# Moving the experts' tiles to other distances from the weights, modulo 256 bytes

## The chip, the cores and the metric

The kernel runs on one core of one Trainium2 chip. The metric is device time in microseconds (us) of one execution. Five units work side by side and meet only at semaphores: TensorE (PE; its weight load, LDWEIGHTS, is shown apart as PEld), VectorE (DVE), ScalarE (ACT), GpSimd (POOL) and SyncE (SP), which issues most of the DMA transfers. Tiles lie in the on-chip memory SBUF, 128 partitions wide; a tile's address is its byte offset inside a partition. Matmul results go to a second memory, `ps` in the code. In a matmul one operand, 128 by 128, is loaded first and stays (the stationary one); the other streams past it column by column (the moving one).

## The reference: what is computed

A decoder trunk of two layers is run for 256 prompt tokens and 32 sample tokens, 288 in all, of width 1024. Each layer mixes (gated DeltaNet heads beside a Conformer convolution) and then has a feed-forward part: layer 0 a dense SwiGLU of width 2816, layer 1 a choice of two among eight experts, each a SwiGLU of width 3584. The change touches only the experts:

```
def swiglu(x, wg, wu, wd):
    return (jax.nn.silu(x @ wg) * (x @ wu)) @ wd

# moe_swiglu(h, ...), cut
logits = h @ w_r + b_r;  probs = softmax(logits)
top_p, top_e = lax.top_k(probs, 2);  top_p = top_p / sum(top_p)
...                                   # assignments sorted by expert, blocks of 128 rows
yb = lax.map(expert_block, (xb, block_e))        # swiglu(xblk, wg[e], wu[e], wd[e])
contrib = yb[dest] * sp[:, None]
return segment_sum(contrib, stok, num_segments=n_tok)
```

All inputs are 32-bit floats.

## The kernel before, in words

**Weights.** All large weights come as units of 128 x 2048 floats (1 MB). SyncE loads them in a fixed order into six buffers `raw`. For most of them the product is taken in three parts, to keep 32-bit accuracy with the fast matmul type float32r: ScalarE rounds a unit into `whi` (L687), VectorE puts the remainder raw - whi into `wlo` (L1061), and TensorE adds up three products: high by high, high by low and low by high. `whi` and `wlo` have three buffers each.

**Before the experts.** In the input projection of layer 0's later units and of layer 1's, and in the dense feed-forward (L1702 to L1704), the weights are the stationary operand and the tokens' tiles `h_hi`, `h_lo`, `act_hi`, `act_lo` move, 288 columns at a time. Their 288-column slices start every 1152 bytes, so that they stand alternately at 0 and at 128 modulo 256. Other projections (L2048, L1885) and the sums of squares for the norms (L1747, stationary operand: the block of ones in `con`) use plain 32-bit matmuls of 288 columns.

**The experts.** Here the roles are turned round. For each expert, `gather` (L2173) fetches its rows: a 0/1 matrix `pe_sel` picks rows of `tok_hi` and `tok_lo` into `xe`, which is transposed and split into `ht_hi[q]` and `ht_lo[q]` (q changes with the expert). Then 42 units follow in the order g, g, u, u, d, d. In the loop of L2241 each unit gives four groups of three matmuls: the stationary operand is a 128 x 128 slice of the experts' rows, the moving one a slice of 512 columns of `whi` or `wlo`:

```
mm(ps[:, bank, :], a_hi[:, a], whi[u % NSPLIT][:, w], ...)    # L2244
mm(ps[:, bank, :], a_hi[:, a], wlo[u % NSPLIT][:, w], ...)    # L2245
mm(ps[:, bank, :], a_lo[:, a], whi[u % NSPLIT][:, w], ...)    # L2246
```

For g and u units `a_hi`, `a_lo` are `ht_hi[q]`, `ht_lo[q]`; for d units they are `at_hi[c % 2]`, `at_lo[c % 2]`, where c counts seven blocks of 512 hidden columns. Between them stand silu(g) (`sge`), the gated product (`ae`), its transposes (L2221) and its split into `at_hi` (ACT, L1031) and `at_lo` (DVE, L1632). The previous expert's result `ye_hi`, `ye_lo` is scattered back to the tokens through `pt_sel` (L2206, L2207) and added to `facc` (L1620). That is 8 experts of 42 units: 336 units and 4032 matmuls of 512 columns.

**What sets the order.** Every engine's program is written out by hand, with semaphores; there is no planner. TensorE needs a unit's `wlo` (semaphore `lo_split`), ScalarE a free `whi` (`unit_used`) and a landed `raw`.

**Addresses.** `at(name, offset, ...)` places a tile at a byte offset, `keep` packs tiles one behind the other. `raw`, `whi` and `wlo` are packed first, 8192 bytes each. `r0`, from which the experts' tiles are counted, lies 86272 bytes behind the first `whi`, and 86272 is 337 x 256. So an offset of `r0 + n` stands at n modulo 256 from the weights. All the experts' tiles have multiples of 256 there but `pos_e`, which stands at 128. `con`, which holds the constants, stands at 32. Slices taken from the tiles for a weight load are 512 bytes apart and those of the weights 2048 bytes, so they keep their tile's remainder.

Of the kernel before, what the change touches and what calls it, by code (L numbers as in the profile page):

```python
# [27 lines left out]
F32R = mybir.dt.float32r  # L28
# [6 lines left out]
P = 128  # L35
D = 1024
# [4 lines left out]
T = TP + TS  # L41
# [224 lines left out]
def program(nc, units, x_in, c_in, par_in, const_in, gdn_in, qst_in, cst_in,  # L266
            y_out, gdnp_out, gdns_out, qst_out, cst_out):
    ctx = ExitStack()
    with ctx:
# [5 lines left out]
        def at(name, offset, cols, dt=F32):  # L275
            return nc.alloc_sbuf_tensor_at(name, [P, cols], dt, offset=offset)
# [23 lines left out]
        r0 = cursor[0]  # L300
# [51 lines left out]
        act_hi = at("act_hi", r0 + 18432, FT * T, F32R)  # L352
        act_lo = at("act_lo", r0 + 43776, FT * T, F32R)

        tok_hi = at("tok_hi", r0 + 36864, 3 * D, F32R)
        tok_lo = at("tok_lo", r0 + 49152, 2 * D, F32R)
        facc = at("facc", r0 + 61440, KD * T)

        ht_hi = [at(f"ht_hi{i}", r0 + 70656 * i, D, F32R) for i in range(2)]
        ht_lo = [at(f"ht_lo{i}", r0 + 70656 * i + 4096, D, F32R) for i in range(2)]  # L360
        xe = at("xe", r0 + 78848, D)
        sge = [at(f"sge{i}", r0 + 8192 + 2048 * i, 512) for i in range(2)]
        ae = [at(f"ae{i}", r0 + 12288 + 2048 * i, 512) for i in range(2)]
        at_hi = [at(f"at_hi{i}", r0 + 16384 + 16128 * i, 512, F32R) for i in range(2)]
        at_lo = [at(f"at_lo{i}", r0 + 18432 + 16128 * i, 512, F32R) for i in range(2)]
        ye_hi = at("ye_hi", r0 + 20480, D, F32R)
        ye_lo = at("ye_lo", r0 + 24576, D, F32R)
        pe_sel = at("pe_sel", r0 + 28672, 3 * P, F32R)
        pt_sel = [at(f"pt_sel{i}", r0 + 30208 + i * 52736, T, F32R) for i in range(2)]
        pos_e = at("pos_e", r0 + 31360, T, F32R)  # L370
        ones_r = at("ones_r", r0 + 84480, P, F32R)
        wgt_parts = at("wgt_parts", r0 + 85248, 6 * NE, F32R)
        assert r0 + 89088 <= base + room, (base + room - r0)
# [2013 lines left out]
```

## Time and profile before

| | |
|---|---|
| time of the kernel, median of 3 runs | 1764.25 us (1761.23 to 1768.3) |
| the profiled execution | 1764.47 us |
| its span, first to last instruction | 1762.7 us |
| PE / PEld / DVE / ACT busy | 1719.2 / 1442.9 / 1370.3 / 1033.9 us |
| first and last of the experts' L2244 start at | 758.8 and 1744.4 us |
| granted TensorE clock, mean | 0.983 of 2.4 GHz |

The page shows one execution. Matmuls overlap in the pipeline and the end of each is modelled, so the time from one matmul's start to the next one's start says how fast TensorE goes; the duration printed for one does not. A PE that is "busy" throughout can still be slower than it might be.

### The profile page before, as it was taken

The numbers are of one execution on the slowest core, as the hardware profiler recorded it, in microseconds if no ns is written. First come the engines' busy times: TensorE is split into PE (matmuls) and PEld (weight loads), VectorE is DVE, ScalarE is ACT, GpSimd is POOL, SyncE is SP. The second block draws the span as 40 slices with busy tenths as digits, with TensorE's granted clock in tenths as the row PEclk, the third lists the DMA queues.
The fourth block names the chain that finished last, engine by engine and source line by source line (L and its number), as shares of the span: only waits on it lengthen the run. The fifth ranks groups of instructions, "written<-read, shape, count | busy, mean of one in ns | idle before, by whom it ended". The sixth has DMA issues, their size and how long they took to land.

```text
span 1762.7 us, 25478 instructions
## 1 busy us (share of the span) xinstructions
PE 1719.2 (98%) x9464; PEld 1442.9 (82%) x9464; DVE 1370.3 (78%) x1627; ACT 1033.9 (59%) x989; POOL 77.7 (4%) x97
## 2 busy tenths in 40 slices
PE   6999999999999999799999999999999999999997
PEld 3878978999978798578888888888888888888886
DVE  2698565554348975678898898998988988988998
ACT  3345424443333544167777777777777777777775
POOL 0122100000011130100000000000000000000000
PEclk9999999999999999899999999999999999999999
DMA  9776047444476510379999999999999999999997
GB/s 384 297 307 217 25 173 291 166 164 168 144 283 267 202 56 31 120 278 344 358 362 351 359 368 347 359 356 339 376 359 353 350 360 344 376 346 371 351 366 268
DMA packets 73386, 499.49 MB, mean 283 GB/s; under 512 B 8096, under 2 KB 8224, under 8 KB 15296
## 3 DMA queue, kind: packets, MB, share of 16 engines
q1 hardware_dynamic: 69728, 481.16, 72.3%
q0 software_dynamic: 3552, 16.87, 2.5%
q8 instruction: 72, 1.18, 0.3%
q14 instruction: 34, 0.28, 0.0%
HBM read 485.95 MB, written 12.05 MB: 283 GB/s over the span
## 4 chain that ended last, share of the span: by engine, by line
PE 91%; DVE 6%; DMA 2%; issue 1%; ACT 0%; SPq 0%; DVEq 0%
PE ps L2244 17%; PE ps L2246 17%; PE ps L2245 17%; PE ps L1702 5%; PE ps L1704 5%; PE ps L1703 5%; PE ps L1885 3%; PE ps L2048 3%; PE ps L1713 2%; DMA raw<-units 2%; DVE yc L1131 1%; PE ps L2221 1%; PE ps L2188 1%; PE ps L1723 1%; PE ps L1793 1%; PE ps L1808 1%
## 5 line engine op out<-in xcount | busy, mean ns | idle before, releaser
L1061 DVE TENSOR_TENSOR wlo<-raw,whi 128x2048 fp32r<-128x2048 f32 x384 | 876.6, 2291 | 184.6 <-ACT whi L687 184.5
L687 ACT ACTIVATE whi<-raw 128x2048 fp32r<-128x2048 f32 x384 | 735.6, 1918 | 256.4 <-PE ps L2246 203.3
L2244 PE MATMUL ps<-whi,ht_hi 128*128 128x512 f32 x896 | 355.5, 397 | 1.7 <-DVE ht_lo L1606 1.7
L2246 PE MATMUL ps<-whi,ht_lo 128*128 128x512 f32 x896 | 349.3, 390 | 0.0
L2245 PE MATMUL ps<-wlo,ht_hi 128*128 128x512 f32 x896 | 349.3, 390 | 0.0
L2246 PEld LDWEIGHTS ps<-whi,ht_lo 128*128 128x128 f32 x896 | 168.1, 188 | 35.8
L2244 PEld LDWEIGHTS ps<-whi,ht_hi 128*128 128x128 f32 x896 | 168.3, 188 | 34.9 <-issue 1.9
L2245 PEld LDWEIGHTS ps<-wlo,ht_hi 128*128 128x128 f32 x896 | 168.5, 188 | 31.5
L2244 PE MATMUL ps<-whi,at_hi 128*128 128x512 f32 x448 | 175.2, 391 | 0.0
L2246 PE MATMUL ps<-whi,at_lo 128*128 128x512 f32 x448 | 174.4, 389 | 0.0
L2245 PE MATMUL ps<-wlo,at_hi 128*128 128x512 f32 x448 | 174.4, 389 | 0.0
L1702 PE MATMUL ps<-h_hi,whi 128*128 128x288 f32 x560 | 167.2, 299 | 0.0
L1703 PE MATMUL ps<-h_lo,whi 128*128 128x288 f32 x560 | 165.2, 295 | 0.0
L1704 PE MATMUL ps<-h_hi,wlo 128*128 128x288 f32 x560 | 164.7, 294 | 0.0
L1702 PEld LDWEIGHTS ps<-h_hi,whi 128*128 128x128 f32 x560 | 104.9, 187 | 9.8 <-issue 9.7
L1704 PEld LDWEIGHTS ps<-h_hi,wlo 128*128 128x128 f32 x560 | 105.5, 188 | 0.0
L1703 PEld LDWEIGHTS ps<-h_lo,whi 128*128 128x128 f32 x560 | 105.1, 188 | 0.1
L1131 DVE SCALAR_TENSOR_TENSOR yc<-cpad,par,yc 128x256 f32<-128x256 f32 x240 | 103.9, 506 | 0.0
L2246 PEld LDWEIGHTS ps<-whi,at_lo 128*128 128x128 f32 x448 | 84.1, 188 | 17.8
L2244 PEld LDWEIGHTS ps<-whi,at_hi 128*128 128x128 f32 x448 | 84.1, 188 | 16.7
L2245 PEld LDWEIGHTS ps<-wlo,at_hi 128*128 128x128 f32 x448 | 84.1, 188 | 16.6
L2048 PE MATMUL ps<-hf,raw 128*128 128x288 f32 x352 | 91.6, 421 | 2.8 <-DVE hf L1111 2.8
(347 smaller groups left out, 2012.9 us busy)
## 6 DMA issues: line engine op xcount, KB each, us to landing
raw<-units SPq DMA_DIRECT2D x447, 1024.0 KB, 6.4
raw<-units SPq DMA_DIRECT2D x16, 512.0 KB, 5.9
sst<-gdn_in POOLq DMA_DIRECT2D x8, 512.0 KB, 6.2
gdns_out<-sst POOLq DMA_DIRECT2D x8, 512.0 KB, 4.3
qst_out<-qpad POOLq DMA_DIRECT2D x2, 1890.0 KB, 10.4
cst_out<-cpad POOLq DMA_DIRECT2D x2, 1116.0 KB, 13.1
x<-x_in SPq DMA_DIRECT2D x1, 1152.0 KB, 9.1
y_out<-hf SPq DMA_DIRECT2D x2, 576.0 KB, 2.9
```

What stands on the lines that cost most here:

```text
L687: act.activation(whi[s % NSPLIT][:, :], raw[u % NRAW][:, :], ACT.Copy).then_inc(hi_split, 1)
L1061: dve.tensor_tensor(wlo[s % NSPLIT][:, :], raw[unit_of(s) % NRAW][:, :], whi[s % NSPLIT][:, :].bitcast(F32), ALU.subtract).then_inc(lo_spl ...
L1131: dve.scalar_tensor_tensor(y, cp3[:, c, j:j + TP], w, y, ALU.mult, ALU.add).then_inc(tap_prompt, 1)
L1702: mm(out, w_hi, x_hi, start=start, stop=False)
L1703: mm(out, w_hi, x_lo, start=False, stop=False)
L1704: return mm(out, w_lo, x_hi, start=False, stop=stop)
L1713: last = mm(ps[32 * k:32 * k + 32, bank, :], cst3[:, 4 * half + k], raw[u % NRAW][:, k * 512:(k + 1) * 512], start=(half == 0), stop=(half ...
L1885: last = mm(ps[:, bank, 0:T], raw[u % NRAW][:, w], part, start=(k == 0), stop=(k == 3))
L2048: last = mm(ps[:, bank, 0:T], raw[u % NRAW][:, w], hf3[:, k], start=(k == 0), stop=(k == KD - 1))
L2244: mm(ps[:, bank, :], a_hi[:, a], whi[u % NSPLIT][:, w], start=(first and i == 0), stop=False)
L2245: mm(ps[:, bank, :], a_hi[:, a], wlo[u % NSPLIT][:, w], start=False, stop=False)
L2246: last = mm(ps[:, bank, :], a_lo[:, a], whi[u % NSPLIT][:, w], start=False, stop=(end and i == 3))
```

## The change

The offsets of the expert stage's tiles (14 names, some with two buffers) become others; nothing else is edited. The sizes stay, and so does the order of every engine's instructions: on PE, DVE, ACT, POOL and SP the two programs have the same instructions in the same order. Tiles that stay are `facc`, `ones_r`, `wgt_parts` and all tiles of the stages before the experts.

```
--- before.py
+++ after.py
@@ -352,22 +352,22 @@
         act_hi = at("act_hi", r0 + 18432, FT * T, F32R)
         act_lo = at("act_lo", r0 + 43776, FT * T, F32R)
 
-        tok_hi = at("tok_hi", r0 + 36864, 3 * D, F32R)
-        tok_lo = at("tok_lo", r0 + 49152, 2 * D, F32R)
+        tok_hi = at("tok_hi", r0 + 37888, 3 * D, F32R)
+        tok_lo = at("tok_lo", r0 + 50176, 2 * D, F32R)
         facc = at("facc", r0 + 61440, KD * T)
 
-        ht_hi = [at(f"ht_hi{i}", r0 + 70656 * i, D, F32R) for i in range(2)]
-        ht_lo = [at(f"ht_lo{i}", r0 + 70656 * i + 4096, D, F32R) for i in range(2)]
-        xe = at("xe", r0 + 78848, D)
-        sge = [at(f"sge{i}", r0 + 8192 + 2048 * i, 512) for i in range(2)]
-        ae = [at(f"ae{i}", r0 + 12288 + 2048 * i, 512) for i in range(2)]
-        at_hi = [at(f"at_hi{i}", r0 + 16384 + 16128 * i, 512, F32R) for i in range(2)]
-        at_lo = [at(f"at_lo{i}", r0 + 18432 + 16128 * i, 512, F32R) for i in range(2)]
-        ye_hi = at("ye_hi", r0 + 20480, D, F32R)
-        ye_lo = at("ye_lo", r0 + 24576, D, F32R)
-        pe_sel = at("pe_sel", r0 + 28672, 3 * P, F32R)
-        pt_sel = [at(f"pt_sel{i}", r0 + 30208 + i * 52736, T, F32R) for i in range(2)]
-        pos_e = at("pos_e", r0 + 31360, T, F32R)
+        ht_hi = [at(f"ht_hi{i}", r0 + (192, 70880)[i], D, F32R) for i in range(2)]
+        ht_lo = [at(f"ht_lo{i}", r0 + (4384, 75104)[i], D, F32R) for i in range(2)]
+        xe = at("xe", r0 + 79200, D)
+        sge = [at(f"sge{i}", r0 + 8512 + 2048 * i, 512) for i in range(2)]
+        ae = [at(f"ae{i}", r0 + 12608 + 2048 * i, 512) for i in range(2)]
+        at_hi = [at(f"at_hi{i}", r0 + (16800, 33280)[i], 512, F32R) for i in range(2)]
+        at_lo = [at(f"at_lo{i}", r0 + (19168, 35328)[i], 512, F32R) for i in range(2)]
+        ye_hi = at("ye_hi", r0 + 21216, D, F32R)
+        ye_lo = at("ye_lo", r0 + 25312, D, F32R)
+        pe_sel = at("pe_sel", r0 + 29408, 3 * P, F32R)
+        pt_sel = [at(f"pt_sel{i}", r0 + (30944, 83296)[i], T, F32R) for i in range(2)]
+        pos_e = at("pos_e", r0 + 32096, T, F32R)
         ones_r = at("ones_r", r0 + 84480, P, F32R)
         wgt_parts = at("wgt_parts", r0 + 85248, 6 * NE, F32R)
         assert r0 + 89088 <= base + room, (base + room - r0)
```

Distance from the weights, modulo 256 bytes:

| tile | before | after |
|---|---|---|
| ht_hi[0], ht_lo[0] | 0, 0 | 192, 32 |
| ht_hi[1], ht_lo[1] | 0, 0 | 224, 96 |
| at_hi[0], at_lo[0] | 0, 0 | 160, 224 |
| at_hi[1], at_lo[1] | 0, 0 | 0, 0 |
| ye_hi, ye_lo | 0, 0 | 224, 224 |
| pt_sel[0], pt_sel[1] | 0, 0 | 224, 96 |
| pe_sel, pos_e | 0, 128 | 224, 96 |
| xe, sge[0], sge[1], ae[0], ae[1] | 0 | 96, 64, 64, 64, 64 |
| tok_hi, tok_lo | 0, 0 | 0, 0 |

All the new offsets are multiples of 32.

## Rows read from the trace of the kernel before

**Rows 1.** The page, parts 1 and 2: busy time; clock, DMA and GB/s by slice

```profile
PE 1719.2 (98%) x9464; PEld 1442.9 (82%) x9464; DVE 1370.3 (78%) x1627; ACT 1033.9 (59%) x989; POOL 77.7 (4%) x97
...
PEclk9999999999999999899999999999999999999999
DMA  9776047444476510379999999999999999999997
GB/s 384 297 307 217 25 173 291 166 164 168 144 283 267 202 56 31 120 278 344 358 362 351 359 368 347 359 356 339 376 359 353 350 360 344 376 346 371 351 366 268
```

**Rows 2.** The page, part 4: the chain that ended last

```profile
PE 91%; DVE 6%; DMA 2%; issue 1%; ACT 0%; SPq 0%; DVEq 0%
PE ps L2244 17%; PE ps L2246 17%; PE ps L2245 17%; PE ps L1702 5%; PE ps L1704 5%; PE ps L1703 5%; PE ps L1885 3%; PE ps L2048 3%; PE ps L1713 2%; DMA raw<-units 2%; DVE yc L1131 1%; PE ps L2221 1%; PE ps L2188 1%; PE ps L1723 1%; PE ps L17
```

**Rows 3.** Stretches: busy us (x instructions) by engine, PE clock, DMA share, GB/s

```profile
core 0: us, PE busy (x) PEld busy (x) DVE busy (x) ACT busy (x) POOL busy (x), PEclk, DMA share, GB/s
300.00:400.00 100.00, 100.00 (x752) 100.00 (x752) 48.91 (x48) 47.53 (x51) 0.00 (x0) 1.00 0.47 168
575.00:596.00 21.00, 21.00 (x88) 16.43 (x88) 20.93 (x48) 8.55 (x27) 3.49 (x4) 1.00 0.34 112
1596.00:1607.00 11.00, 11.00 (x50) 9.13 (x49) 9.78 (x8) 7.68 (x4) 0.00 (x0) 1.00 0.93 357
...
757.00:1735.00 978.00, 976.35 (x4493) 808.22 (x4493) 872.99 (x604) 716.85 (x489) 0.00 (x0) 1.00 0.94 354
```

**Rows 4.** The page, part 5: busy us, mean ns of one, idle us before

```profile
L1061 DVE TENSOR_TENSOR wlo<-raw,whi 128x2048 fp32r<-128x2048 f32 x384 | 876.6, 2291 | 184.6 <-ACT whi L687 184.5
L687 ACT ACTIVATE whi<-raw 128x2048 fp32r<-128x2048 f32 x384 | 735.6, 1918 | 256.4 <-PE ps L2246 203.3
L2244 PE MATMUL ps<-whi,ht_hi 128*128 128x512 f32 x896 | 355.5, 397 | 1.7 <-DVE ht_lo L1606 1.7
...
L2244 PEld LDWEIGHTS ps<-whi,ht_hi 128*128 128x128 f32 x896 | 168.3, 188 | 34.9 <-issue 1.9
...
L2244 PE MATMUL ps<-whi,at_hi 128*128 128x512 f32 x448 | 175.2, 391 | 0.0
...
L2048 PE MATMUL ps<-hf,raw 128*128 128x288 f32 x352 | 91.6, 421 | 2.8 <-DVE hf L1111 2.8
```

**Rows 5.** Timeline, PE, an undisturbed stretch of the expert stage

```profile
start us, us, engine line op out<-in xcount [idle before <-releaser]
...
1596.44 0.39 PE L2246 MATMUL ps<-whi,ht_lo 128*128 128x512 f32 x1
1596.67 0.39 PE L2244 MATMUL ps<-whi,at_hi 128*128 128x512 f32 x1
1596.89 0.39 PE L2245 MATMUL ps<-wlo,at_hi 128*128 128x512 f32 x1
1597.12 0.39 PE L2246 MATMUL ps<-whi,at_lo 128*128 128x512 f32 x1
...
1598.71 0.39 PE L2244 MATMUL ps<-whi,at_hi 128*128 128x512 f32 x1
```

**Rows 6.** Timeline, PE, in the dense feed-forward part's stage

```profile
299.83 0.29 PE L1703 MATMUL ps<-h_lo,whi 128*128 128x288 f32 x1
299.97 0.29 PE L1704 MATMUL ps<-h_hi,wlo 128*128 128x288 f32 x1
...
301.04 0.29 PE L1703 MATMUL ps<-h_lo,whi 128*128 128x288 f32 x1
```

**Rows 7.** Timeline, PE, 32-bit matmuls: an input projection, and the sums of squares of a norm

```profile
574.10 23.20 PE L2048 MATMUL ps<-hf,raw 128*128 128x288 f32 x95
...
488.35 4.04 PE L1747 MATMUL ps<-sqx,con 128*128 128x288 f32 x16
```

**Rows 8.** Timeline, PE, the largest spacing that is common in the expert stage

```profile
783.16 0.40 PE L2244 MATMUL ps<-whi,at_hi 128*128 128x512 f32 x1
783.40 0.39 PE L2245 MATMUL ps<-wlo,at_hi 128*128 128x512 f32 x1
```

## The prediction

> **What bounds the kernel now.** Read the busy table and the slices first: PE is busy for 98% of the span, and the granted clock is at nine tenths or more in all slices but one [rows 1]. The chain of waits says the same with more weight: 91% of it is PE, and the three expert matmul lines L2244 to L2246 are 51% of the whole span [rows 2]. So the question is only how fast these matmuls follow each other. The groups by line show 0.0 to 1.7 us of idle time before them, while DVE (L1061) and ACT (L687) have 184.6 and 256.4 us of idle before their splits, most of it for each other or for PE [rows 4]. In the stretch of the experts, 978 us, PE is busy for 976.35, DVE for 873 (89%), and the DMA engines for 94% [rows 3]. PE binds; DMA and DVE are 6 and 11% behind it, which matters if PE gets faster.
>
> A busy PE may still be slowed by how it reads its operands, and this change can act only there. So take spacings, start to start, not the printed durations.
> - Experts, float32r, 512 columns: 1596.44 to 1598.71 us is ten spacings, 227 ns each [rows 5]; the 11 us stretch around it agrees, (11.00 + 0.39) / 50 = 228 [rows 3].
> - Token projections and the dense part, float32r, 288 columns: (100.00 + 0.29) / 752 = 133.4 ns [rows 3].
> - The two differ by 93.6 ns over 224 columns, 0.418 ns a column, which is 2.4 GHz at a granted clock of 1.00 [rows 3]. At that rate 512 columns take 213.3 ns and 288 take 120.0. What remains, 13.7 and 13.4 ns, is a fixed part per matmul, the same for both lengths.
> - Plain 32-bit matmuls of 288 columns take two passes, 240 ns: L2048 has (23.20 - 0.42) / 94 = 242.3 ns, and the norms' L1747 (4.04 - 0.42) / 15 = 241.3 [rows 7]. The fixed part is 1 to 2 ns.
>
> So float32r pays about 11 ns per matmul that 32-bit matmuls do not pay. In both cases a new 128 x 128 operand is loaded per matmul, beside the running one (the spacing is shorter than the 188 ns that a load is shown with [rows 4]). Either the 11 ns are part of how float32r operands are exchanged, or the load takes read cycles from a moving stream that reads at full rate. In the second case the distance of the two addresses could count.
>
> **The change part by part.**
>
> *Instructions.* None is added, removed or moved on any engine or queue, and no semaphore changes. Cost 0. No DMA writes or reads a moved tile.
>
> *Weight loads of the expert matmuls.* Of 4032, the 3 x 896 from `ht_hi`, `ht_lo` get a new distance, and of the 3 x 448 from `at_hi`, `at_lo` those of blocks c = 0, 2, 4, 6, four of seven, 768. That makes 2688 + 768 = 3456; the 576 of c = 1, 3, 5 keep distance 0. What does a distance do? The trace has three comparisons.
> - In the 288-column stretches the tokens' slices stand alternately at 0 and 128 from the weights, and rows of both follow each other in 299.83 to 301.04 us: nine spacings of 134 ns with no odd one [rows 6]. At 128 a float32r matmul costs what it does at 0.
> - L1747 takes its stationary operand at 32 modulo 256 against a moving one at 0 or 128; L2048 has both at 0 or 128. 241.3 and 242.3 ns [rows 7]: 32 and its fellow 160 (128 further) cost nothing there. [...]
> - The fixed part does not grow with the moving length (13.4 at 288, 13.7 at 512). And the loads run beside ACT and DVE operations that are busy for 70% and 89% of the time in the same memory (7.68 and 9.78 of 11 us in that stretch), without the spacing leaving 227 [rows 3, 5].
>
> Value taken: 0. Bounds: downward, the whole excess over the 32-bit fixed part goes, 13.5 - 2 = 11 ns by 3456 = 38 us. Upward, no row shows float32r at another distance; the largest spacing that is common in the stage is 0.24 us [rows 8], 13 ns over 227, and by 3456 that is 45 us. I take 0 because the nearest rows, float32r at 0 and 128, show no difference.
>
> The row has 13.4 to 13.7 ns above the columns' own time. [...]
>
> *Transposes, gather, scatter.* `ae` and `xe` move to 64 and 96, `ye`, `pe_sel` and `pt_sel` to 224 or 96. These are 32-bit transposes and a few short float32r matmuls: 4493 matmuls are counted in the stage [rows 3], of which 4032 are the main ones, so about 460. At the same 11 ns either way they are 5 us; I take 0.
>
> *ACT and DVE.* Their large splits (2291 and 1918 ns [rows 4]) use only `raw`, `whi`, `wlo`, which stay. The small ones on `sge`, `ae`, `at`, `ye` get new addresses, all multiples of 32. Even 5% on them would be covered: DVE has 978 - 873 = 105 us free in the stage, ACT more [rows 3]. Cost 0, and some 2 us at most where one stands before a matmul that waits (L2244 has 1.7 us of such idle time [rows 4]).
>
> Sum: 0 on the profiled execution's 1764.47 us, which is the median of 1764.25 within 0.3 us. Forecast 1764 us.
>
> **The rivals.**
>
> *The distance 0 is a clash now, and the new distances avoid it.* [...] Against: no difference between 0 and 128, so it would need a pattern that repeats every 128 bytes or less. All gone: 1764 - 38 = 1726 us. Could DMA follow? 336 units of 1.049 MB in 986 us are 357 GB/s; in 948 us they would be 372, and the first slice shows 384 [rows 1]. DVE would be at 93%. So both allow it, hardly more. Half of the tiles well placed: 1745 us. Chance 0.22.
>
> *The distance 0 is the good one, and others clash.* One mechanism on the other side: at equal remainders the load's read and the moving read use different moments or banks; shifted by 32 to 224 bytes they meet, and the load holds back the moving stream. Place: L2244 to L2246, from 759 to 1744 us of the span. It decides from the first nanosecond, as PE has no slack there. Price: up to 13 ns by 3456, 45 us, 1809 us; with half of the distances bad 22 us, 1787. For: the before is at a uniform 0, so nothing in it tells what a true offset of 32 or 96 does to float32r. Against: the 128 rows. Chance 0.18.
>
> *Only some distances matter and cancel.* The seven new values could have both signs; the result would look like no change, with the spacing of `ht` units differing from that of `at` units. It is part of the forecast's band, time 1755 to 1772.
>
> **How the numbers follow.** No change 0.60, first rival 0.22, second 0.18. A measurement of this kernel can tell about 0.5%, 9 us, from no change. The forecast's own range is 1757 to 1772 us (runs before: 1761.23 to 1768.3). Together with half of each rival it becomes 1738 to 1788, outside of which I leave the full size of either, some 0.14. Faster by over 0.5%: 0.22; within: 0.60; slower: 0.18.
>
> **What would show it right or wrong.** Right: ten spacings in an undisturbed run of L2244 to L2246 are again 2.27 us, alike for `ht_hi[0]` (192), `ht_hi[1]` (224), `at_hi[0]` (160) and the unmoved `at_hi[1]`; PE's stretch of the experts again 986 us. Wrong on the faster side: a spacing near 216 ns for moved tiles beside 227 for c = 1, 3, 5, and DMA's share rising to 0.97. Wrong on the slower side: over 227 for moved tiles alone. If the time changed while all spacings stayed, the cause would be outside of the loads, in ACT or DVE operations on moved tiles, and their durations would show it.

## The result: 0.9% slower, and the spacing of the expert matmuls shows where

| | before | after |
|---|---|---|
| time, median of 5 runs | 1764.25 us (1761.23 to 1769.56) | 1780.57 us (1776.63 to 1788.39) |
| ratio, 95% interval | | 1.009 (1.0067 to 1.0113) |
| first to last L2244 of the experts, profiled execution | 758.8 to 1744.4, 985.7 us | 769.2 to 1768.4, 999.2 us |
| the same, sum of the 4032 main spacings | 927.1 us | 940.3 us |

The forecast of no change was wrong; the second rival (distance 0 is the good one) happened, in the experts' stage at 13.5 us of its highest price of 45. The ratios here and below compare fast executions: one of the twelve of a kernel below, 2161.2 us at a granted clock of 0.745, was slow and is left out. The page of the changed kernel, parts 1, 2, 4 and 5, answers to [rows 1, 2, 4]:

```profile
PE 1742.2 (98%) x9464; PEld 1450.0 (81%) x9464; DVE 1372.3 (77%) x1627; ACT 1034.0 (58%) x989; POOL 79.4 (4%) x97
...
PEclk8999999999989998899999999999999999999999
DMA  9776047444377510378999998989999999999996
...
PE 92%; DVE 4%; DMA 2%; issue 1%; ACT 0%; SPq 0%; DVEq 0%
...
L2244 PE MATMUL ps<-whi,ht_hi 128*128 128x512 f32 x896 | 357.1, 399 | 1.6 <-DVE ht_lo L1606 1.6
L2246 PE MATMUL ps<-whi,ht_lo 128*128 128x512 f32 x896 | 353.6, 395 | 0.0
L2245 PE MATMUL ps<-wlo,ht_hi 128*128 128x512 f32 x896 | 352.7, 394 | 0.0
```

Nothing waits more than it did: the idle time before the expert matmuls is 1.6 us against 1.7, the chain is as much PE's. All engines have the same counts. Fewer matmuls fit into a stretch of the same length, and DMA and DVE do less in it too. The 200 us from 1100 us on lie inside the experts' stage in both; columns as in [rows 3], before and then after:

```profile
1100.00:1300.00 200.00, 200.00 (x921) 165.91 (x920) 179.81 (x122) 146.59 (x99) 0.00 (x0) 1.00 0.95 359
```

```profile
1100.00:1300.00 200.00, 200.00 (x909) 163.51 (x908) 177.23 (x120) 145.02 (x99) 0.00 (x0) 1.00 0.92 353
```

921 against 909 matmuls is 1.3%, at a granted clock of 1.00 in both: the engine is as "busy", and slower. Only the matmuls themselves got longer, and the page shows that faintly, since its durations are modelled (399 ns against 397). The timeline shows it plainly, start to start. First the unmoved pair `at_hi[1]`, `at_lo[1]` in the last expert of the changed kernel, first and last L2244 of eight:

```profile
1723.36 0.39 PE L2244 MATMUL ps<-whi,at_hi 128*128 128x512 f32 x1
...
1728.12 0.39 PE L2244 MATMUL ps<-whi,at_hi 128*128 128x512 f32 x1
```

Then the moved pair `at_hi[0]`, `at_lo[0]` (160 and 224), again eight, and `ht` of the same expert (224 and 96), three:

```profile
1763.51 0.39 PE L2244 MATMUL ps<-whi,at_hi 128*128 128x512 f32 x1
...
1768.36 0.39 PE L2244 MATMUL ps<-whi,at_hi 128*128 128x512 f32 x1
```

```profile
1684.37 0.39 PE L2244 MATMUL ps<-whi,ht_hi 128*128 128x512 f32 x1
1685.07 0.39 PE L2244 MATMUL ps<-whi,ht_hi 128*128 128x512 f32 x1
1685.77 0.39 PE L2244 MATMUL ps<-whi,ht_hi 128*128 128x512 f32 x1
```

Seven turns of three matmuls take 4.76 us, 680 ns a turn, for the unmoved pair, and 4.85 us, 693 ns, for the moved one; `ht[1]` takes 700. The unmoved pair is a control inside the same execution: same lines, same clock, same traffic. From here on the measure is the turn: the time from one L2244 to the next inside a unit. A unit has four groups and so three turns. The first is left out, since the unit's first matmul often follows other work of PE (means of 704.9 ns before, 711.5 after); the figure given is the median over the second and third turns of a pair, 672 turns in all. Before, all pairs have 680 ns; after, `ht[0]` (192, 32) has 687, `ht[1]` (224, 96) 700, `at[0]` (160, 224) 693, `at[1]` (0, 0) 680.

The sum of the spacings grew by 13.2 us, the stage by 13.5, the medians of the times by 16.3; with the interval of the ratio that is 12 to 20 us, so the stage accounts for it. The further 10.4 us by which this profiled execution is longer stand ahead of the experts, where the program is the same. The experts' first L2244 starts between 752.1 and 769.3 us in the profiled executions of this study, and late also where the layout is that of before in effect (769.3 below, with all distances kept). The granted clock goes with it. The traces have two levels of it, 1.00 and 0.50, and at 0.50 PE works at half speed: in the kernel before, the 32-bit matmuls of L2048 start every 480 ns from 506.4 to 510.3 us, at 0.50, and every 242 or 243 ns behind that, at 1.00. Ahead of the experts TensorE was at 0.50 for 58.0 us in the kernel before, 81.9 us in the changed one and 78.5 us in the one with all distances kept. If PE was busy all that time, half of the excess is lost: by this estimate 11.9 and 10.2 us, against the 10.4 and 10.5 us measured. It is rough: the last kernel below, all main tiles at 192, also has 81.9 us at 0.50, and its first L2244 is 6.2 us late. From 200 to 300 us, for instance, the granted clock is 0.98, 0.95 and 0.91, and 666, 642 and 619 matmuls fit in. In the experts' stage it is 1.00 in every kernel here. Why the clock differs where the program is the same is not shown. So single times are not compared here to better than 1%; stages, turns and ratios of several executions are.

### The profile page after: what moved, and what is told of

It reads as the page before. It is cut to its first block, busy times and chain, and to the rows that moved or that the text cites. A ratio compares the mean times of both kernels' runs of the same rounds, so it can differ in the third digit from the quotient of the medians.

```text
span 1786.6 us, 25478 instructions
## 1 busy us (share of the span) xinstructions
PE 1742.2 (98%) x9464; PEld 1450.0 (81%) x9464; DVE 1372.3 (77%) x1627; ACT 1034.0 (58%) x989; POOL 79.4 (4%) x97
## 4 chain that ended last, share of the span: by engine, by line
PE 92%; DVE 4%; DMA 2%; issue 1%; ACT 0%; SPq 0%; DVEq 0%
PE ps L2246 17%; PE ps L2245 17%; PE ps L2244 17%; PE ps L1702 5%; PE ps L1704 5%; PE ps L1703 5%; PE ps L2048 4%; PE ps L1885 3%; PE ps L1713 2%; DMA raw<-units 2%; PE ps L2221 1%; PE ps L2188 1%; PE ps L1723 1%; DVE yc L1131 1%; PE ps L1793 1%; PE ps L1808 1%
## 5 line engine op out<-in xcount | busy, mean ns | idle before, releaser
L1061 DVE TENSOR_TENSOR wlo<-raw,whi 128x2048 fp32r<-128x2048 f32 x384 | 877.6, 2290 | 195.9 <-ACT whi L687 194.4
L687 ACT ACTIVATE whi<-raw 128x2048 fp32r<-128x2048 f32 x384 | 735.1, 1916 | 264.8 <-PE ps L2246 213.7
L2244 PE MATMUL ps<-whi,ht_hi 128*128 128x512 f32 x896 | 357.1, 399 | 1.6 <-DVE ht_lo L1606 1.6
L2246 PE MATMUL ps<-whi,ht_lo 128*128 128x512 f32 x896 | 353.6, 395 | 0.0
L2245 PE MATMUL ps<-wlo,ht_hi 128*128 128x512 f32 x896 | 352.7, 394 | 0.0
L2246 PEld LDWEIGHTS ps<-whi,ht_lo 128*128 128x128 f32 x896 | 168.1, 188 | 38.6
L2244 PEld LDWEIGHTS ps<-whi,ht_hi 128*128 128x128 f32 x896 | 168.3, 188 | 37.1 <-issue 1.9
L2245 PEld LDWEIGHTS ps<-wlo,ht_hi 128*128 128x128 f32 x896 | 168.3, 188 | 35.5
L2244 PE MATMUL ps<-whi,at_hi 128*128 128x512 f32 x448 | 176.6, 394 | 0.0
L2246 PE MATMUL ps<-whi,at_lo 128*128 128x512 f32 x448 | 175.8, 392 | 0.0
L2245 PE MATMUL ps<-wlo,at_hi 128*128 128x512 f32 x448 | 175.4, 391 | 0.0
L1702 PE MATMUL ps<-h_hi,whi 128*128 128x288 f32 x560 | 167.7, 299 | 0.0
L1704 PE MATMUL ps<-h_hi,wlo 128*128 128x288 f32 x560 | 164.9, 295 | 0.0
L1702 PEld LDWEIGHTS ps<-h_hi,whi 128*128 128x128 f32 x560 | 105.4, 188 | 10.1 <-issue 10.0
L1704 PEld LDWEIGHTS ps<-h_hi,wlo 128*128 128x128 f32 x560 | 105.7, 189 | 0.0
L2246 PEld LDWEIGHTS ps<-whi,at_lo 128*128 128x128 f32 x448 | 84.1, 188 | 19.3
L2245 PEld LDWEIGHTS ps<-wlo,at_hi 128*128 128x128 f32 x448 | 84.2, 188 | 18.0
L2244 PEld LDWEIGHTS ps<-whi,at_hi 128*128 128x128 f32 x448 | 84.2, 188 | 17.6
L2048 PE MATMUL ps<-hf,raw 128*128 128x288 f32 x352 | 95.1, 432 | 3.0 <-DVE hf L1111 3.0
## 6 DMA issues: line engine op xcount, KB each, us to landing
qst_out<-qpad POOLq DMA_DIRECT2D x2, 1890.0 KB, 10.5
```

The lines of the kernel that those rows point to most:

```text
L687: act.activation(whi[s % NSPLIT][:, :], raw[u % NRAW][:, :], ACT.Copy).then_inc(hi_split, 1)
L1061: dve.tensor_tensor(wlo[s % NSPLIT][:, :], raw[unit_of(s) % NRAW][:, :], whi[s % NSPLIT][:, :].bitcast(F32), ALU.subtract).then_inc(lo_spl ...
L1702: mm(out, w_hi, x_hi, start=start, stop=False)
L1704: return mm(out, w_lo, x_hi, start=False, stop=stop)
L2048: last = mm(ps[:, bank, 0:T], raw[u % NRAW][:, w], hf3[:, k], start=(k == 0), stop=(k == KD - 1))
L2244: mm(ps[:, bank, :], a_hi[:, a], whi[u % NSPLIT][:, w], start=(first and i == 0), stop=False)
```

## Experiments

Each of these kernels is the kernel before or the changed one with other offsets. Seven of them were executed once (1769.78 to 1791.85 us), and only their stages and turns are read; the last three have ratios of 6 to 11 executions against 13 or 17 of the kernel before. In those that place single pairs, the small tiles (xe, sge, ae, ye, pe_sel, pt_sel, ones_r, tok) stand at 0 modulo 256 from `whi` and pos_e at 128, only spaced a little wider.

### All addresses moved, no distance changed

```diff
         raw = [keep(f"raw{i}", UNIT) for i in range(NRAW)]
+        cursor[0] += 96
         whi = [keep(f"whi{i}", UNIT, F32R) for i in range(NSPLIT)]
```

> The kernel before, with everything behind the raw buffers moved up by 96 bytes, so that all distances between weights and tiles stay and only the addresses change. Theory A: 680 ns per three expert matmuls and 133.3 per 288-column matmul, as before, time 1764 us within 0.5%. Theory C: the three take 690 to 700 ns, some 1780 us.

All pairs have 680 ns, the stage takes 986.1 us, the 288-column turns 400 ns as before. The one time, 1775.39 us, is over what was expected; its stage of the experts starts at 769.3 us, 10.5 us late, with the 78.5 us at 0.50 told of above. (One line more in the program: L2245 here is L2244 before.) The timeline, first and last of eight for `at[0]`, 4.76 us:

```profile
1750.61 0.39 PE L2245 MATMUL ps<-whi,at_hi 128*128 128x512 f32 x1
...
1755.37 0.39 PE L2245 MATMUL ps<-whi,at_hi 128*128 128x512 f32 x1
```

So an address by itself costs nothing; theory C falls.

### The weights moved, the tiles not

```diff
+        cursor[0] += 96
         whi = [keep(f"whi{i}", UNIT, F32R) for i in range(NSPLIT)]
...
+        cursor[0] += 160
         r0 = cursor[0]
```

> The kernel before, with whi and wlo moved up by 96 bytes and the experts' and tokens' tiles by 256, so that the tiles keep their address modulo 256 and the weights do not: the experts' tiles stand at 160 from the weights, and the weights at 96 or 224 from the moving tokens' tiles in L1702 to L1704. Theory A: the expert matmuls cost what ht[0] at 160 costs in the run with 160, above 680 ns for three; the 288-column ones go above 133.3 ns too, at up to 16 cycles each some 140 ns. Theory C: 680 ns for the experts, since their tiles' addresses are as before.

All pairs have 700 ns, in 642 of 672 turns exactly, and the stage takes 1007.7 us. The experts' tiles have the addresses modulo 256 that they had; of the operands of these matmuls only `whi` and `wlo` moved. (L2246 and L1704 here are L2244 and L1702 before.) `at[0]`, seven turns in 4.90 us, and 288-column matmuls, five turns in 2.01 us:

```profile
1767.00 0.39 PE L2246 MATMUL ps<-whi,at_hi 128*128 128x512 f32 x1
...
1771.90 0.39 PE L2246 MATMUL ps<-whi,at_hi 128*128 128x512 f32 x1
```

```profile
329.99 0.30 PE L1704 MATMUL ps<-h_hi,whi 128*128 128x288 f32 x1
330.39 0.29 PE L1704 MATMUL ps<-h_hi,whi 128*128 128x288 f32 x1
330.79 0.30 PE L1704 MATMUL ps<-h_hi,whi 128*128 128x288 f32 x1
...
332.00 0.29 PE L1704 MATMUL ps<-h_hi,whi 128*128 128x288 f32 x1
```

Together with the kernel above this shows that the distance between the two operands counts, not the place of either. At 288 columns it counts too, but not as expected: turns of 395 and 405 ns alternate for `h` (96 and 224 from the moving slice, in turn), with a mean of 400.4, and turns of 400 and 407 ns for `act`, with a mean of 403.3; both have 400 before. The expected 140 ns per matmul, 420 a turn, did not come. (Its 16 cycles are a third of the 20 ns that the dearest pair of the changed kernel has over 680.)

### The map: which distance costs what

Three kernels of the same kind; the lines of the first one for the four pairs:

```diff
-        ht_hi = [at(f"ht_hi{i}", r0 + 70656 * i, D, F32R) for i in range(2)]
-        ht_lo = [at(f"ht_lo{i}", r0 + 70656 * i + 4096, D, F32R) for i in range(2)]
+        ht_hi = [at(f"ht_hi{i}", r0 + (32, 70720)[i], D, F32R) for i in range(2)]
+        ht_lo = [at(f"ht_lo{i}", r0 + (4128, 74816)[i], D, F32R) for i in range(2)]
...
-        at_hi = [at(f"at_hi{i}", r0 + 16384 + 16128 * i, 512, F32R) for i in range(2)]
-        at_lo = [at(f"at_lo{i}", r0 + 18432 + 16128 * i, 512, F32R) for i in range(2)]
+        at_hi = [at(f"at_hi{i}", r0 + (16992, 33664)[i], 512, F32R) for i in range(2)]
+        at_lo = [at(f"at_lo{i}", r0 + (19040, 35712)[i], 512, F32R) for i in range(2)]
```

> All tiles of the experts stand at 0 modulo 256 from the weights again, but the four pairs of stationary tiles each stand at one distance, the same for high and low part: ht[0] at 32, ht[1] at 64, at[0] at 96, at[1] at 128. Theory A (the distance between the operand that is loaded and the moving one costs by itself): three matmuls (L2244 to next L2244, steady) take more than 680 ns for 32, 64 and 96, between 685 and 705 as in the changed kernel, and 680 for 128, since 0 and 128 were alike at 288 columns. Theory B (what costs is the jump between two distances, high and low part differing): 680 ns for all four pairs. Theory C (only the tile's own address counts, modulo 256): as A here.

> All other tiles at 0. Distance of high and low part: ht[0] 192 and 192, ht[1] 224 and 224, at[0] 0 and 128, at[1] 0 and 64. Theory A (each load costs by its own distance, additive over the three matmuls): 192 and 224 alike cost 695 to 703 ns per three, as 32, 64, 96, 128 and 160 did (699, 700, 703, 696, 700); with the high part at 0, two loads of three are free, so 0 and 128 cost 680 + 16/3 = 685 and 0 and 64 cost 687. Theory D (what counts is where each load meets the stream, which depends on the load before it as well): mixed pairs may lie anywhere, below 680 too.

> All other tiles at 0. High and low part: ht[0] 0 and 32, ht[1] 0 and 192, at[0] 32 and 0, at[1] 0 and 160. Theory A: 680 + 19/3 = 686 for 0 and 32, 686 for 0 and 192, 680 + 2 x 19/3 = 693 for 32 and 0, 687 for 0 and 160. Theory D: no such order, and 0 and 32 against 32 and 0 do not stand at one third and two thirds.

The three kernels give these turns, in steps of 32 bytes. That 0 and 128 were alike at 288 columns, on which the first expectation rests for 128, is measured: 134 ns in nine spacings with both in turn [rows 6].

| high, low | turn, ns | | high, low | turn, ns |
|---|---|---|---|---|
| 0, 0 | 680 | | 0, 32 | 700 |
| 32, 32 | 699 | | 0, 64 | 693 |
| 64, 64 | 700 | | 0, 128 | 693 |
| 96, 96 | 703 | | 0, 160 | 700 |
| 128, 128 | 696 | | 0, 192 | 694 |
| 160, 160 | 700 | | 32, 0 | 691 |
| 192, 192 | 687 | | 192, 32 | 687 |
| 224, 224 | 700 | | 224, 96 | 700 |
| | | | 160, 224 | 693 |

(160 is from the kernel with moved weights and from the one below; the last three mixed ones are from the changed kernel.) A pair is called even here when high and low part stand at one distance. Theory B falls with the first column: even pairs still cost. Theory A has the sign right for every even pair but 128, which it put at 680, and not the size of the mixed ones: with the high part at 0 two of three loads should be free, 686, yet 0, 32 and 0, 160 cost the full 700, and 0, 64, 0, 128 and 0, 192 have 693 or 694. An even 192, expected at 695 to 703, has 687. What is left is theory D, which forecasts no numbers. Since even 128 costs 16 ns, the pattern does not repeat after 128 bytes; tiles at other multiples of 256 than before (`at_hi[0]` 512 bytes further on, below) keep the 680. Last, 0 and 160 in the timeline, seven turns in 4.89 us:

```profile
1725.82 0.40 PE L2244 MATMUL ps<-whi,at_hi 128*128 128x512 f32 x1
...
1730.71 0.40 PE L2244 MATMUL ps<-whi,at_hi 128*128 128x512 f32 x1
```

### Which two operands meet

`wlo` is moved from `whi` as well, to ask whether the load is disturbed by the moving operand that it runs beside or by that of its own matmul. In the timeline of the kernel before, the load for an L2245 starts at 1595.99 us and takes 0.19 us; the L2244 ahead of it starts at 1595.99 too, and the L2245 itself at 1596.21. So a load lies beside the matmul ahead of its own.

```diff
-        wlo = [keep(f"wlo{i}", UNIT, F32R) for i in range(NSPLIT)]
-        x = keep("x", KD * T)
+        cursor[0] += 64; wlo = [keep(f"wlo{i}", UNIT, F32R) for i in range(NSPLIT)]
+        cursor[0] += 192; x = keep("x", KD * T)
```

The pairs are placed by the same four lines as above.

> Now wlo is moved too, by 64 bytes from whi; all tiles but the main ones stand at 0 from whi. High and low part from whi: ht[0] 0 and 64, ht[1] 0 and 0, at[0] 64 and 64, at[1] 192 and 64. Theory E (what counts is the distance between the operand being loaded and the moving operand of the matmul that runs beside the load: high part beside whi, twice, low part beside wlo): ht[0] has 0, 0 and 64 - 64 = 0 and takes 680 ns for three; ht[1] has 0, 0, -64 and takes more, 685 to 700. Theory F (what counts is the distance inside one matmul, its own stationary against its own moving operand): ht[0] has 0, -64, 64 and takes 690 to 700, like the pair 0 and 64 before (693).

> The same with wlo moved by 128 bytes from whi. High and low part from whi: ht[0] 0 and 128, ht[1] 128 and 128, at[0] 0 and 0, at[1] 192 and 192. Theory E: ht[0] has 0, 0, 0 and takes 680 ns for three; at[0] has 0, 0, -128 and takes about the 693 of the pair 0 and 128. Theory F: ht[0] has 0, -128, 128 and takes 690 to 700. Below 680 in any pair would mean that 0 everywhere isn't the best layout; I expect none.

In the order `ht[0]`, `ht[1]`, `at[0]`, `at[1]`, with 64: 693, 696, 699 and 693 ns. With 128: 693 (mostly 705 and 682), 687, 700 and 691. `ht[0]`, for which theory E wanted 680, has 693 in both, and `at[0]` has 700 where it wanted about 693. Theory E falls in this form. Theory F holds its numbers, but with what the map says of the mixed pairs it isn't shown either. No pair's median is below 680. The 288-column turns fell, though, from a mean of 399.9 ns to 396.9 with `wlo` at 64 and to 398.2 at 128: over 736 turns some 2 us and 1 us, less than can be timed. So for those matmuls one remainder for all is not the best layout.

### The main tiles back, the small ones left moved

The diff is against the changed kernel:

```diff
-        ht_hi = [at(f"ht_hi{i}", r0 + (192, 70880)[i], D, F32R) for i in range(2)]
-        ht_lo = [at(f"ht_lo{i}", r0 + (4384, 75104)[i], D, F32R) for i in range(2)]
+        ht_hi = [at(f"ht_hi{i}", r0 + (0, 70656)[i], D, F32R) for i in range(2)]
+        ht_lo = [at(f"ht_lo{i}", r0 + (4096, 74752)[i], D, F32R) for i in range(2)]
...
-        at_hi = [at(f"at_hi{i}", r0 + (16800, 33280)[i], 512, F32R) for i in range(2)]
-        at_lo = [at(f"at_lo{i}", r0 + (19168, 35328)[i], 512, F32R) for i in range(2)]
+        at_hi = [at(f"at_hi{i}", r0 + (16896, 33280)[i], 512, F32R) for i in range(2)]
+        at_lo = [at(f"at_lo{i}", r0 + (18944, 35328)[i], 512, F32R) for i in range(2)]
```

> The changed kernel with ht_hi, ht_lo, at_hi and at_lo at distance 0 again, and xe, sge, ae, ye, pe_sel, pt_sel and pos_e where the change put them. Theory A: these main matmuls carry the whole cost; three take 680 ns everywhere, the stage of the experts is within 2 us of 986, and the time is within 0.3% of the kernel before, ratio 0.997 to 1.003. Rival: the small tiles (transposes, scatter, ACT and DVE operations) carry a part of it, ratio 1.003 to 1.006 and a stage of 989 to 993 us.

Ratio 1.0008 (0.9992 to 1.0024). All four pairs have 680 ns, the stage takes 987.8 us. `at[0]` again, 4.76 us:

```profile
1739.92 0.39 PE L2244 MATMUL ps<-whi,at_hi 128*128 128x512 f32 x1
...
1744.68 0.39 PE L2244 MATMUL ps<-whi,at_hi 128*128 128x512 f32 x1
```

The loss is gone with four tile names. What the other ten names could cost is the 2.1 us between 985.7 and 987.8, under what can be timed. Of these, 1.7 lie in the main spacings themselves (928.8 against 927.1 us), although the main tiles are where they were; whether the small tiles' places cause that is not shown. ACT's and DVE's operations on them are as they were: in the stage, L1632 has 684 ns and L1644 has 685 here, both 684 before.

### The dose

All eight main tiles at one distance, 160 in the first kernel and 192 in the second, in the same four lines as above; of the first:

```diff
-        ht_hi = [at(f"ht_hi{i}", r0 + 70656 * i, D, F32R) for i in range(2)]
+        ht_hi = [at(f"ht_hi{i}", r0 + (160, 70816)[i], D, F32R) for i in range(2)]
```

> All eight main tiles (ht and at, high and low) at 160, all others at 0. If the time follows from the spacings alone, three matmuls take 700 ns everywhere, as with the weights moved by 96, the stage of the experts takes 1007 to 1008 us against 985.7, and the time goes up by 22 us, ratio 1.0125, 1.011 to 1.014. Rival: if the position of the tile itself matters beside the distance, three take something else than 700.

> All eight main tiles at 192. ht[0] at 192 had 687 ns for three; if that holds for the others, the stage takes about 985.7 + 7 x 1.344 - 2 = 993 us and the ratio is 1.004, 1.003 to 1.006. Rival: the 687 is a property of ht[0]'s place and at[] or ht[1] at 192 cost about 700, ratio 1.008 or more.

At 160: 700 ns in all pairs, stage 1007.2 us, ratio 1.013 (1.0106 to 1.0154). At 192: 687 ns in all pairs, stage 992.3 us, ratio 1.005 (1.0034 to 1.0067). Both as expected. `at[0]` of either, seven turns in 4.90 and in 4.80 us:

```profile
1761.97 0.39 PE L2244 MATMUL ps<-whi,at_hi 128*128 128x512 f32 x1
...
1766.87 0.39 PE L2244 MATMUL ps<-whi,at_hi 128*128 128x512 f32 x1
```

```profile
1752.50 0.39 PE L2244 MATMUL ps<-whi,at_hi 128*128 128x512 f32 x1
...
1757.30 0.39 PE L2244 MATMUL ps<-whi,at_hi 128*128 128x512 f32 x1
```

So the turn is a property of the distance, not of the tile, and the time follows it: 20, 7 and 0 ns per turn give 1.3%, 0.5% and nothing. The stage grows by 21.5 us at 160, and not by the 27 us of 20 ns for each of 1344 turns, because turns behind other work of PE are above 680 already before: the first turns of the units go from a mean of 704.9 ns to 718.2, by 13.

One rival is in the same traces. ACT writes `whi` and DVE writes `wlo` while PE reads, so the distance might count between their writes and a load. At 160, 129 of the 672 turns pass with ACT's split L687 running all along and DVE's L1061 not at all, and 15 the other way round. Both groups have a median of 700 ns, like the 266 turns with both. Before, 105 and 22 such turns have 680. So neither write by itself is needed for the cost; a turn with neither does not occur.

## Why the prediction was wrong

**What binds.** Right. PE binds before and after, DMA and DVE have room (in the 200 us above a DMA share of 0.95 and 0.92, DVE busy for 90% and 89%), and a change of the spacing goes straight into the time. The spacing was also the right thing to read, and the signs named for the slower side (over 227 ns for moved tiles alone) are what the trace shows.

**The step that failed.** "I take 0 because the nearest rows, float32r at 0 and 128, show no difference" [rows 6]. The term "weight loads of the expert matmuls" was put at 0 and measured 13.2 us: 7, 20 and 13 ns per three matmuls for the three moved pairs, 0 for the pair that stayed. The time, 1780.57 us, lies outside the forecast's own 1757 to 1772 us and inside the wide 1738 to 1788. The rows were true and did not carry over. They are 288-column matmuls in which the tokens move and 0 and 128 alternate; with 512 columns and the experts' rows loaded, an even 128 costs 16 ns per turn. Which of the two, the length or the exchanged roles, makes the difference was not tested. Of the five new distances of the main tiles (32, 96, 160, 192, 224) the trace before had none with float32r. The value should have been left open between its bounds.

**The 32-bit rows** [rows 7]. "Two passes" is a reading of the time, 242 ns for 288 columns. L1838, 32-bit matmuls of 512 columns (from 138.8 us in the kernel before), has spacings of 429 ns at a granted clock of 1.00, so a column more costs 0.83 ns, twice the 0.418 of float32r; no run shows the passes. That 32 and 160 cost nothing there was right as read, but of 32-bit matmuls: with float32r at 512 columns an even 32 costs 19 ns a turn and an even 160 costs 20. The runs fit for the 32-bit transposes: `ae` and `xe` at 64 and 96 cost at most part of 2.1 us in the kernel with the main tiles back. What spares the 32-bit matmuls is not shown.

**The size of the rival.** Its place (L2244 to L2246), its sign and its absence of slack were right. Its price of up to 13 ns for each of 3456 matmuls was too high: 13.2 us over 3456 is 3.8 ns. The dearest distance measured is 96, 23 ns per three. Its case of "half of the distances bad" was wrong too: all three moved pairs are worse, and all seven even distances are. That some distances could be better than 0 and cancel the others did not happen. The rival's mechanism, reads that use different moments or banks at equal remainders, is a supposition; no run shows it.

**The first rival** (the fixed 13.5 ns are a clash that a distance could avoid) found no support: in the 25 combinations that were tried (8 even, 9 mixed, 8 with `wlo` moved) none has a median below 680. In cycles of 2.4 GHz, one for each of the prediction's 0.418 ns a column (that is all that shows the "full rate" of the moving stream), the turn of 680 ns is 1632 for 1536 columns, 32 over per matmul; 687 is 38 over, 700 is 48. Whether the 32 are themselves such a clash that these placements don't avoid stays open, and so does the choice between an exchange of operands and read cycles that a load takes.

**The small tiles, ACT and DVE at 0.** Right to within 2.1 us. The count behind the term was low: the stretch ends at 1735 us, ahead of the last main matmuls, so that 503 of its 4493 are others, not 460. At 11 ns that is 6 us in place of 5.

**What stays open.** Which two accesses meet. It is a relation between stationary and moving tile modulo 256, shown from both sides. The kernel with the main tiles at 160 differs from the one before, modulo 256 bytes, in the place of those tiles alone, and the one with the weights moved keeps their addresses; both have 700 ns in place of 680, and with everything moved by 96 it is 680. But it isn't a sum over the three loads, and the distance to the operand beside which a load runs doesn't give it (theory E). Nor is it tied to one of the three matmuls: with all main tiles at 160 the spacings follow each other as 231, 232 and 237 ns, and the long one stands behind L2244 in some units, behind L2245 or L2246 in others. What sets its place is not shown.

## What to carry to other kernels

Where dense float32r matmuls with a new stationary tile each bind, compare the spacing from start to start with columns at the granted clock, and try stationary and moving tiles at the same remainder modulo 256 bytes; here, at 512 columns, each other even distance cost 1 to 3.4% of the matmul stream. At 288 columns with the weights loaded it did not pay: moving `wlo` by 64 bytes took 0.8% off those turns. A tile that keeps its place is a control inside the same trace. The granted clock ahead of the changed stage can differ between two executions that do the same work there, so compare stage by stage. And a price read from rows of another length and another role is a bound, not a value.

## What the runs showed of the hardware that was not expected

- The spacing of back-to-back float32r matmuls of 512 columns is 226.7 ns with stationary and moving tiles at one remainder modulo 256 bytes, and 229 to 234 ns at every other even distance in steps of 32. Tiles at odd and at even multiples of 256 bytes from the weights have the same 680 ns per three. The address itself doesn't matter (680 ns per three with everything moved by 96).
- 128 bytes are not neutral at 512 columns (696 ns per three against 680), though they are at 288 columns (400 and 400), where a distance of 96 or 224 gives 395 or 405 for `h` and 400 or 407 for `act`.
- Of the even distances, 192 is the mildest, 687 ns, with spacings of 226, 229 and 232 ns in turn.
- The granted clock ahead of the experts differs between executions where instructions and layout up to there are the same: of the eight such profiled ones, the one with 54.6 us at 0.50 starts the experts at 756.9 us, and the one with 85.3 us at 768.1.
